# Feed-forward pairs of seven products: the token factor moved behind the down product, and a new order of work inside a pair

## The reference, cut to what matters

```python
def _rmsnorm(x, g):
    x32 = x.astype(jnp.float32)
    y = x32 * lax.rsqrt(jnp.mean(x32 * x32, axis=-1, keepdims=True) + RMS_EPS)
    return (y * g.astype(jnp.float32)).astype(x.dtype)

def _swiglu(x, w_gate, w_up, w_down):
    return (jax.nn.silu(x @ w_gate) * (x @ w_up)) @ w_down

x = x + 0.5 * _swiglu(_rmsnorm(x, ffn1_norm[l]), ffn1_w_gate[l], ffn1_w_up[l], ffn1_w_down[l])
...
x = x + 0.5 * _swiglu(_rmsnorm(x, ffn2_norm[l]), ffn2_w_gate[l], ffn2_w_up[l], ffn2_w_down[l])
```

## Time and profile before

| | |
|---|---|
| median of 3 runs | 3309.1 us (3308.97 to 3309.43) |
| the profiled execution's own time | 3310.0 us |
| its span | 3308.2 us |
| PE busy | 3125.8 us, 94% of the span |
| DVE busy | 2197.6 us, 66% |
| ACT busy | 1384.5 us, 42% |
| POOL busy | 1213.2 us, 37% |
| of POOL's: `gate_scale` (L864), 80 times | 122.0 us |

### The profile page before, as it was taken

How to read it: one execution, slowest core, us unless ns; L and a number is a source line. 1 busy time by engine, 2 the same in 40 slices (tenths; PEclk the granted TensorE clock), 3 DMA queues, 4 the chain that set the end, 5 groups by cost and what they waited for, 6 DMA issues and landing times.

```text
span 3308.2 us, 48205 instructions
## 1 busy us (share of the span) xinstructions
PE 3125.8 (94%) x17808; PEld 2629.3 (79%) x17808; DVE 2197.6 (66%) x3151; ACT 1384.5 (42%) x2328; POOL 1213.2 (37%) x899
## 2 busy tenths in 40 slices
PE   7898999989999898999989999999999999999999
PEld 6888876788887888876688887768788886688887
DVE  6849578685876949578695875456747555567474
ACT  5434336443434424336442433464424335444242
POOL 4636427562645626417562642023000213220003
PEclk9999999999999999999999999999999999999999
DMA  4245341223232233331223233212333322123332
GB/s 118 84 130 140 91 121 46 77 84 102 84 93 79 80 106 90 88 82 45 77 83 102 83 94 104 77 39 71 98 93 95 107 75 61 45 77 105 88 100 82
DMA packets 528498, 289.17 MB, mean 87 GB/s; under 512 B 13630, under 2 KB 520225, under 8 KB 528314
## 3 DMA queue, kind: packets, MB, share of 16 engines
q1 hardware_dynamic: 523706, 273.40, 28.9%
q0 software_dynamic: 4608, 13.30, 1.4%
HBM read 284.38 MB, written 10.02 MB: 89 GB/s over the span
## 4 chain that ended last, share of the span: by engine, by line
PE 50%; POOL 17%; issue 17%; DVE 9%; ACT 4%; DMA 1%; DVEq 0%; ACTq 0%; POOLq 0%; SPq 0%
PE bank L2332 29%; PE bank L2350 5%; POOL ws_raw L859 4%; POOL gated L864 3%; POOL s_two L849 3%; POOL s_two L846 3%; PE bank L2637 3%; POOL ws_raw L855 2%; PE bank L2747 2%; PE bank L2367 2%; PE bank L2435 2%; PE bank L2789 2%; PE bank L2812 1%; PE bank L2570 1%; ACT w_hi L1031 1%
## 5 line engine op out<-in xcount | busy, mean ns | idle before, releaser
L1031 ACT ACTIVATE w_hi<-w_raw 128x1024 fp32r<-128x1024 f32 (+2 forms) x311 | 359.0, 1155 | 1002.6 <-PE bank L2332 614.0
L2385 PE MATMUL bank<-h_hi,ws 128*128 128x256 f32 x2560 | 507.6, 291 | 127.1 <-DVE prod L1834 84.4
L1614 DVE TENSOR_TENSOR w_lo<-w_raw,w_hi 128x1024 fp32r<-128x1024 f32 (+2 forms) x279 | 423.7, 1519 | 287.6 <-ACT w_hi L1031 287.5
L2385 PEld LDWEIGHTS bank<-h_hi,ws 128*128 128x128 f32 x2560 | 415.5, 194 | 155.6 <-DVE prod L1834 97.6
L2332 PE MATMUL bank<-h_hi,w_hi 128*128 128x512 f32 (+1 forms) x1140 | 452.3, 397 | 13.8 <-DVE w_lo L1614 10.0
L2332 PE MATMUL bank<-h_hi,w_lo 128*128 128x512 f32 (+1 forms) x1140 | 444.6, 390 | 0.0
L2332 PE MATMUL bank<-h_lo,w_hi 128*128 128x512 f32 (+1 forms) x1128 | 439.9, 390 | 0.0
L2385 PE MATMUL bank<-h_lo,ws 128*128 128x256 f32 x1280 | 365.6, 286 | 0.0
L2385 PE MATMUL bank<-t_hi,ws 128*128 128x256 f32 x1920 | 361.2, 284 | 2.7 <-ACT gate_sum L1229 2.7
L2332 PE MATMUL bank<-act_hi,w_hi 128*128 128x512 f32 x836 | 325.3, 389 | 0.0
L2332 PE MATMUL bank<-act_hi,w_lo 128*128 128x512 f32 x836 | 325.2, 389 | 0.0
(11 more groups left out here) (392 smaller groups left out, 6890.9 us busy)
## 6 DMA issues: line engine op xcount, KB each, us to landing
w_raw<-in_ffn_w_down_dram SPq DMA_DIRECT2D x64, 704.0 KB, 4.6
w_raw<-in_ffn_w_in_dram SPq DMA_DIRECT2D x88, 512.0 KB, 3.8
raw_g<-in_ffn_w_gate_dram SPq DMA_DIRECT2D x80, 512.0 KB, 4.8
raw_u<-in_ffn_w_up_dram SPq DMA_DIRECT2D x71, 512.0 KB, 3.9
w_raw<-in_ffn_w_out_dram SPq DMA_DIRECT2D x32, 704.0 KB, 4.4
w_raw<-in_w_in_dram SPq DMA_DIRECT2D x34, 512.0 KB, 3.8
w_raw<-in_a_w_qkv_dram SPq DMA_DIRECT2D x24, 512.0 KB, 3.7
w_raw<-in_w_out_dram SPq DMA_DIRECT2D x16, 512.0 KB, 3.7
```

The lines of the kernel that those rows point to most:

```text
L1031: nc.scalar.activation(split_home(c)[0][:, 0:nk, 0:cols], raw[c % 2][:, 0:nk, 0:cols], ACT.Copy).then_inc(hi_ready, 1)
L1614: nc.vector.tensor_tensor(w_low[:, 0:nk, 0:cols], raw[c % 2][:, 0:nk, 0:cols], w_high[:, 0:nk, 0:cols].bitcast(f32), ALU.subtract).then_in ...
L2385: mm = nc.tensor.matmul(dst, w, v, start=(first and k == 0 and n == 0), stop=(k == KH - 1 and n == 2), skip_group_check=True)
```

## The change

1. `gate_scale` is gone from POOL, and the multiplication by `rstd` from `whole_pair`. DVE now waits for silu itself. In exchange `take` of these stages' down units is two DVE instructions: the down result times 0.5 times `rstd` into `down_t`, then `down_t` added to `xres`. The tiles `down_t` lie over `gated` and `prod`.
2. DVE's order in a pair is another: the cross sum stands ahead of the low part of the next `s_two`, `product` is split in two parts (`product_last` directly behind `gate_last`, `product_first` later), and `act_low` stands ahead of `last_low`.
3. ACT's order is another: silu of the pair before stands ahead of the copy of P1, and the high part of `ws_raw` right behind that copy.
4. In `whole_pair` of the second block the low parts of pair 2 stand ahead of the division of the gate, and on ACT the high parts of pair 2 ahead of its silu.

```diff
-            def gate_scale(name, hf, j):
-
-                pool.wait_ge(silu_ready, FF[name] + FH * hf - CONV_FF[name] + 1 + j)
-                nc.gpsimd.tensor_tensor(gated[:, :], gated[:, :], rstd[:, :], ALU.mult).then_inc(gate_ready, 1)
...
@@ ACT, gated_ff
                     if hf == 0:
                         silu(0, 0)
                         product_high(0, 0)
-                        silu(0, 1)
                     raw_high(hf, j0)
                     sums_high(hf, j0, False)
                     if hf == 0:
+                        silu(0, 1)
                         product_high(0, 1)
                     for j in range(j0, FH):
                         more = j + 1 < FH
+                        if j > j0:
+                            silu(hf, j - 1)
                         part_of(hf, j, "P1", gate_sum[j % 2][:, HALF[0]], SUM_D[j % 2])
-                        if j == j0:
-                            sums_high(hf, j, True)
-                        else:
-                            silu(hf, j - 1)
+                        sums_high(hf, j, True)
...
@@ DVE, take
+                    if how == "scaled":
+                        nc.vector.scalar_tensor_tensor(down_t[b][:, :, :], got, 0.5, rstd[:, :].rearrange("p (o n) -> p o n", o=1),
+                                                       ALU.mult, ALU.mult).then_inc(down_scaled, 1)
+                        dve.wait_ge(down_scaled, n + taken + 1)
+                        ins = nc.vector.tensor_tensor(xres[:, DS(n, 1), :], down_t[b][:, :, :], xres[:, DS(n, 1), :], ALU.add)
...
@@ DVE, gated_ff
                         if j > j0:
                             gate_last(hf, j - 1)
-                            sums_low(name, hf, j, True)
+                            product_last(hf, j - 1)
                         gate_first(hf, j)
-                        if j == j0:
-                            sums_low(name, hf, j, True)
-                        else:
-                            product(hf, j - 1)
+                        sums_low(name, hf, j, True)
+                        if j > j0:
+                            product_first(hf, j - 1)
                         if more:
                             raw_low(name, hf, j + 1)
-                        last_low(hf, j)
                         if j > j0:
                             act_low(a0 + j, j - 1)
                         elif hf == 0:
                             token_low(name, 3)
+                        last_low(hf, j)
+                        up_cross(hf, j)
                         if more:
                             sums_low(name, hf, j + 1, False)
                         else:
                             lo(down)
-                        up_cross(hf, j)
```

More of the change, by code:

```diff
@@ L302, in program @@
         norm_t = [put(f"norm_t{i}", [P, T], prob_at + 4 * i * T) for i in range(4)]
+        down_t = [put(f"down_t{i}", [P, 1, T], prob_at + 12 * i * T) for i in range(2)]
         gate_sum = [put(f"gate_sum{i}", [P, T], prob_at + 4 * T * (1 + i)) for i in range(2)]
@@ L1738, in act_low, with output_gemm @@
                                         act_hi[:, DS(jj, 1), :].bitcast(f32), ALU.subtract).then_inc(act_ready, 1)
-            def output_gemm(c, how, name, halves=False, fast=None):
+            def output_gemm(c, how, name, halves=False, fast=None, taken=0):
                 def take(c, n, j=0):
@@ L1745, in take @@
                     dve.wait_ge(mm_done, c + 1 + 2 * j)
-                    if how == "half":
+                    if how == "scaled":
[3 more added lines that the diff above has]
+                        ins = nc.vector.tensor_tensor(xres[:, DS(n, 1), :], down_t[b][:, :, :], xres[:, DS(n, 1), :], ALU.add)
+                    elif how == "half":
                         ins = nc.vector.scalar_tensor_tensor(xres[:, DS(n, 1), :], got, 0.5, xres[:, DS(n, 1), :],
@@ L1852, in whole_pair @@
                         sums_low(name, 0, 2, False)
-                    dve.wait_ge(silu_ready, a0 - CONV_FF[name] + 1 + j)
-                    nc.vector.tensor_tensor(gated[:, :], gated[:, :], rstd[:, :], ALU.mult).then_inc(gate_ready, 1)
+                    divided(c, gate_sum[j][:, :])
                     if j == 1:
                         token_low(name, 2)
-                    dve.wait_ge(gate_ready, a0 - CONV_FF[name] + 1 + j)
+                    dve.wait_ge(silu_ready, a0 - CONV_FF[name] + 1 + j)
                     dve.wait_ge(mm_done, c + 2)
@@ L1890, in gated_ff @@
                             lo(down)
-                        up_cross(hf, j)
                     gate_last(hf, FH - 1)
-                    product(hf, FH - 1)
+                    product_last(hf, FH - 1)
+                    product_first(hf, FH - 1)
                     lo(down + 1)
@@ L1897, in gated_ff @@
                         small_values()
-                    output_gemm(down, "half", name if hf else None, fast=None if hf else name)
+                    output_gemm(down, "scaled", name if hf else None, fast=None if hf else name,
+                                taken=KT * (HALVES * FAST[name] + hf))
             def conv_ff(name):
```

11 lines of the change are left out of this document (4 added, 7 removed).

## The result

| | before | changed |
|---|---|---|
| median | 3309.26 us (4 runs) | 3265.1 us (3263.8 to 3270.2, 4 runs) |
| ratio, 95% interval | | 0.987 (0.985 to 0.989) |
| profiled execution's span | 3308.2 us | 3262.1 us |
| median interval of cross sums | 12.08 us | 11.28 us |
| DVE busy / POOL busy | 2197.6 / 1213.2 us | 2175.4 / 1103.8 us |

What follows compares the result with a forecast made beforehand. It took DVE's cross sum, delayed by port blocking with POOL, to set the 12.08 us pair. Three later stages' 42.6 plus `ffn1_0`'s 8.3 and 0.4 made 51.3 off 3310.0; the median, 0.9 below, 3257.8 (range 3235 to 3300).

Steps and rivals of the forecast that it cites:

- 42 steady intervals of the three later stages: Pairs inside the halves: eleven terms laid out round a pair give 11.30 us, 0.78 less than 12.08; 10.9 us per stage.
- their first intervals: The two first intervals of the halves, 12.98 before, were taken as 11.5: 3.0 us won per later stage.
- their last intervals: The last pair of each half wins nothing and loses 1.1 us, twice per later stage.
- their starts and takes, with the stretch behind the last pair: Per later stage: PE starts the pairs 3.2 us earlier (bounds 2.3 and 4.4); the last take's added instruction costs 0.7.
- `ffn1_0`: The stage outside the three later ones: its first half was to win 8.3 us, its second half 0.4.
- L855 then finds the port with `act_lo`: 0.6 more: Last term of the pair's sum: POOL's L855 waits 0.58 us for DVE's `act_lo` at the shared port (bounds 0 and 1.6).
- The rival of the transfer: A second loop over `raw_u`'s load sets the pairs: landing 3.9 gives 3300 us (chance 0.07), 4.4 gives 3327 (0.06).
- It closes only if L855 asks for the port before `act_lo` does: Condition for the `raw_u` load loop of 12.14 us; the layout had `act_lo` first by about 0.5 us.
- both kinds in one trace: Sign of being wrong: intervals of both loops in one trace, meaning halves or stages split; chance 0.20, about 3283 us.
- the 0.25 for each of nine intervals: Second half of `ffn1_0`: gain of 0.25 us per interval (bounds 0 and 0.78), less 1.8, giving 0.4.
- the take covered: Down units: DVE's waits for PE hide the added 0.69 us instruction in 64 takes; rival, uncovered: 48 us, 3307, chance 0.04.
- its split case: Rival: halves or stages split between both loops, or jump between them; half the gain, about 3283 us, chance 0.20.

## Why the prediction was right, and where it was not

**The sum by its terms**, each from the cross sums of the two profiled executions:

| term | forecast | measured |
|---|---|---|
| 42 steady intervals of the three later stages | 32.7 | 23.7 |
| their first intervals | 9.0 | 11.5 |
| their last intervals | -6.6 | -5.7 |
| their starts and takes, with the stretch behind the last pair | 7.5 | 0.8 |
| `ffn1_0` | 8.7 | 15.7 |
| total (of the unrounded terms) | 51.3 | 46.1 |

**Steady interval.** 11.30 forecast, 11.27 measured, though in 26 of the 42 intervals and not in all stages alike. Each listed piece stands in the rows. The number is right and the reason is not. The failed step is the term "L855 then finds the port with `act_lo`: 0.6 more". It was added like an instruction's duration, but it is a wait, and the length of a wait inside a loop is whatever the rest leaves over. Its bounds were 0 and 1.6, and that 0.58 stood so near the measured 0.56 was luck. In the changed kernel L857 asks at 887.86 and gets the port at 888.42: the way over PE has 0.56 to spare, and by itself would repeat every 10.71 (an estimate: 11.27 less 0.56). A chain that closes at 11.27 in the rows above does not run over PE: the product's first half ends at 883.30, L848, ready at 883.02, ends at 884.50, low part of `ws_raw` 885.58, L851 886.74, low part of `raw_g` 887.82, `act_lo` 888.42, L857 889.57, low part of `raw_u` 890.13, L861 1.14, low part of `s_two` 1.08, sum and scaling 1.13, silu with its way back 0.70, the product's 0.39: 11.27. That chain is read from the timeline. For it speak the 26 intervals that did not follow the landing; against its last step, that any earlier landing opens it, stands the run with 7/8 of `raw_u`. No run proves it whole. What the runs show is that the interval can be moved by the transfer alone, down to 10.28 with half of it, where a loop over PE would have left it at 11.27.

**The rival of the transfer.** Its failed step is "It closes only if L855 asks for the port before `act_lo` does". The pairs run in three ways, told apart by how many of POOL's sums go ahead of the low part of `raw_u`: none (10.3, with half of `raw_u` or with the swap of `act_lo`), L857 (11.27), or L857 and L861 (12.1 to 12.3, the rival's 12.14). By the timelines each keeps itself up: the later `raw_u` is read, the later its buffer is loaded, L848 and L851 run, and `act_lo` comes. One late landing moved a half from the second to the third, and the forecast did give "both kinds in one trace" its place, at 0.20. The forecast did not see the first kind, and it is where the gain lay.

**Spells.** They are the main part of the 9.0 us missing from the steady intervals: the 6 intervals above 11.95 in the later stages are together 7.2 us longer than six of 11.27.

**First and last intervals.** 11.5 us and -5.7, each within 2.5 of the forecast.

**Starts.** The forecast was 3.2 per stage, with 2.3 as the low bound. In the changed kernel:

```profile
642.51 4.51 DVE L1785 TENSOR_TENSOR t_lo<-t_raw,t_hi 128x1024 fp32r<-128x1024 f32 x2
646.95 2.28 DVE L1790 TENSOR_TENSOR ws<-raw_g,ws 128x1024 fp32r<-128x1024 f32 x1
```

The first low part starts 4.44 behind the two `t_lo`'s start and is held itself (2.28 in place of 1.23); before, it came 5.66 behind theirs. The idle time of the earlier trace rows is gone, but `t_lo` took 4.51 in place of 3.41 and the work that the edit saved became time at the port. From the last cross sum of one stage to the first of the next, 1.8, 0.3 and 2.0 us were won; behind the last pair of the program 3.2 were lost. Most of that goes with the cross sum's place: from the last cross sum to the end of the span it is 1356.5 before the change, 1357.4 to 1357.8 in the four other kernels with the cross sum behind the low part that follows it, and 1359.2 to 1359.7 in eight with it ahead, where the count begins at an earlier point. The 0.9 to 1.3 left no run explains.

**`ffn1_0`.** Its first half with the start was to win 8.3 and won 5.5: 3.6 by its start, 1.1 by its intervals, 0.8 behind them. Its second half was to win 0.4 and won 10.3. The failed step is the 0.25 for each of nine intervals: that its transfers land later was taken to hold the gain back. Its intervals are 10.5 to 12.2 there, but for the last.

**Confirmed as they stood:** the cross sum is no longer waited for; the wait for ACT's copies is there in its place (71 times, 0.87 each, forecast 70 at 1.1); `act_lo` mostly at its short length; the take covered; the forecast time within 7.3 us. Of the signs of being wrong, "both kinds in one trace" is there too, so the result lies between the forecast and its split case.

**A row read for more than it shows.** That an instruction with a PSUM input is not stretched was read from the cross sum's 0.41 at 892.11, but POOL stood idle then. The same trace has a fitting row: L1843, with a PSUM input, started at 897.40 beside POOL's L849 and took 0.41. And the second instruction of a take, with two SBUF inputs, took 1.16 in place of 0.69 at 1780.12 of the changed kernel; behind it DVE waited for PE, so it was covered.

**Not asked.** The forecast priced the orders together with the factor and never laid out the factor alone. Laid out from the same kind of rows before its run, though with the changed kernel's result known, it gave 3235 (3224 measured), less than the forecast of the whole change: the sign that part of the bundle costs may have been there in the trace.

## What to carry to other kernels

Where two engines take turns at one resource, a wait for a turn has no length of its own: lay the order out round the loop for every possible order of asking, and see which of them keep themselves up. Where a load is waited for, try the instruction that frees its buffer ahead of one on which nothing is loaded; here that swap was worth 62 us. And price each edit of a bundle alone: here one gained 85 us and the other gave back 41.

## What was not expected of the hardware

- One kernel can run its pairs at different intervals. In the changed kernel most stay at 11.27 and some near 12.2, and two of its spells began with a transfer that took 4.99 and 4.72 from issue to use in place of 4.1; in the run with `product_first` earlier one trace has intervals of 10.1, 11.3 and 12.2.
- Time does not follow a transfer's length: 448 KB (3.7 us) in place of 512 (4.0) changed the time by no more than the runs scatter, 256 KB (2.9) gave 62 us. Halving the transfer took a quarter off its landing.
